# Filler matmuls, a split output projection, and one-hot row picks for the first three experts in a one-core transformer block

## The reference, cut to what matters

```python
mod = silu(c) @ w_ada + b_ada                        # 6 vectors of 1024
h = modulate(rmsnorm(x, norm1_w), shift1, scale1)
proj = h @ w_in                                      # retention q k v g, delta q k v z, a, b
ret = rmsnorm(retention(rotary(q), rotary(k), v)) * silu(g)      # 4 heads of 128
dn  = rmsnorm(gated_delta_rule(conv(q), conv(k), conv(v), g, beta)) * silu(z)   # 4 heads
x = x + gate1 * (concat([ret, dn]) @ w_out)
h2 = modulate(rmsnorm(x, norm2_w), shift2, scale2)
# router: top group of 4, top 2 of its 8 experts (32 experts of 1024 x 512 x 1024)
for each chosen expert e: y = gate * ((silu(h2 @ w1[e]) * (h2 @ w3[e])) @ w2[e])
x = x + gate2 * y;  x = rmsnorm(x)
# second block: pool mixer, then an FFN of 2816 with a causal conv of 3
```

## Time and profile before

| | |
|---|---|
| time, median of 3 runs | 1048.3 us (1047.32 to 1048.72) |
| the profiled execution | 1047.87 us, span 1046.0 us |
| mean granted TensorE clock | 0.948 of full |
| PE busy | 898.8 us (86%) |
| VectorE busy | 365.3 us (35%) |
| ScalarE busy | 199.9 us (19%) |
| moved by DMA | 300.24 MB, mean 287 GB/s |

### The profile page before, as it was taken

The page is one execution under the profiler, slowest core; times in us unless marked ns, Lnnn a source line. Parts: engine busy times, 40 slices in busy tenths (PEclk is TensorE's granted clock), DMA queues, the critical chain, the costliest instruction groups (busy, mean ns, idle before and its releaser), DMA issues.

```text
span 1046.0 us, 11455 instructions
## 1 busy us (share of the span) xinstructions
PE 898.8 (86%) x4665; PEld 545.6 (52%) x4665; DVE 365.3 (35%) x630; ACT 199.9 (19%) x296; POOL 176.1 (17%) x187
## 2 busy tenths in 40 slices
PE   4899999998967979998788887887887279999998
PEld 2687756675433443443233332332332279999987
DVE  1155412232252242221121221211211567888843
ACT  1116212111030000000000000000000335565532
POOL 0001654021020120111101101111001222222300
PEclk9699999997978989999999999999999689999999
DMA  9969227266596999999999999999994884555511
GB/s 344 254 163 262 93 81 238 85 242 258 200 378 227 416 403 401 408 401 401 410 408 409 420 404 401 410 412 414 403 420 192 274 267 151 186 162 187 208 49 41
DMA packets 91348, 300.24 MB, mean 287 GB/s; under 512 B 13451, under 2 KB 37507, under 8 KB 66583
## 3 DMA queue, kind: packets, MB, share of 16 engines
q1 hardware_dynamic: 82295, 286.62, 73.4%
q10 hardware_dynamic: 3872, 8.58, 2.2%
q0 software_dynamic: 5120, 4.22, 1.4%
HBM read 300.43 MB, written 11.53 MB: 298 GB/s over the span
## 4 chain that ended last, share of the span: by engine, by line
PE 60%; DMA 33%; issue 2%; DVE 2%; ACT 2%; POOL 1%; ACTq 0%; POOLq 0%; DVEq 0%
DMA ring<-in_w_dram 19%; DMA arena<-in_w_dram 11%; PE ps L423 9%; PE ps L759 7%; PE ps L843 6%; PE ps L844 6%; PE ps L845 6%; PE ps L412 4%; PE ps L762 4%; PE ps L483 4%; PE ps L782 3%; PE ps L433 2%; PE ps L449 1%; DMA ring<-in_w_ada_dram 1%; PE ps L418 1%
## 5 line engine op out<-in xcount | busy, mean ns | idle before, releaser
L762 PE MATMUL ps<-ring,proj 128*64 128x512 f32 x288 | 129.7, 596 | 25.4 <-DMA ring<-in_w_dram 25.4
L1223 DVE TENSOR_TENSOR proj<-RQ,ps 64x512 f32<-64x512 f32 x32 | 22.1, 690 | 298.2 <-ACT RQ L1562 288.3
L759 PE MATMUL ps<-ring,proj 128*64 128x512 f32 x272 | 124.3, 596 | 0.0
L762 PE MATMUL ps<-arena,proj 128*64 128x512 f32 x224 | 105.4, 619 | 20.3 <-DMA arena<-in_w_dram 20.3
L759 PE MATMUL ps<-arena,proj 128*64 128x512 f32 x240 | 113.9, 617 | 3.6 <-issue 3.6
L1562 ACT ACTIVATE RQ<-ps 64x512 f32<-64x512 f32 x32 | 18.9, 592 | 468.2 <-PE ps L762 468.2
L1792 POOL DMA_INDIRECT pair_scratch<-MX,idx x32 | 32.5, 1014 | 423.7 <-DVE MX L1237 423.7
L843 PE MATMUL ps<-h_h,w_h 128*128 128x256 f32 x352 | 100.4, 285 | 1.6 <-DVE h_l L1319 1.6
L423 PE MATMUL ps<-ring,hT 128*128 128x512 f32 x224 | 100.1, 604 | 0.8 <-ACT hT L1512 0.8
L844 PE MATMUL ps<-h_l,w_h 128*128 128x256 f32 x352 | 100.3, 285 | 0.0
L845 PE MATMUL ps<-h_h,w_l 128*128 128x256 f32 x352 | 100.2, 285 | 0.0
(11 more groups left out here) (286 smaller groups left out, 1374.7 us busy)
## 6 DMA issues: line engine op xcount, KB each, us to landing
ring<-in_w_dram SPq DMA_DIRECT2D x108, 1024.0 KB, 28.2
arena<-in_w_dram SPq DMA_DIRECT2D x84, 1024.0 KB, 27.9
ring<-in_w_ada_dram SPq DMA_DIRECT2D x12, 2048.0 KB, 11.1
ring<-in_ffn_w_in_dram SPq DMA_DIRECT2D x22, 1024.0 KB, 7.8
ring<-in_w_in_dram SPq DMA_DIRECT2D x6, 2048.0 KB, 14.4
ring<-in_ffn_w_out_dram SPq DMA_DIRECT2D x5, 2048.0 KB, 7.6
arena<-in_w_in_dram SPq DMA_DIRECT2D x2, 2048.0 KB, 25.1
ring<-in_w_out_dram SPq DMA_DIRECT2D x2, 2048.0 KB, 7.8
```

What stands on the lines that cost most here:

```text
L759: pe.matmul(ps[0:SLOTS, :], XTe[i % 2][:, k, :], u1[:, k, :], start=(k == 0), stop=(k == 7))
L762: t = pe.matmul(ps[64:64 + SLOTS, :], XTe[i % 2][:, k, :], u3[:, k, :], start=(k == 0), stop=(k == 7))
```

## The change

1. `turn_over(n)` issues n filler matmuls of 128x256 into the next bank. It is put at twelve places: in the first stage, ahead of and between the `ada`, behind the column totals, between the two `logits`, ahead of `rank`, and at two places of `tensor_last`.
2. `column_total` moves 64 columns instead of one.
3. hT is written chunk by chunk, and the first group of `delta_project(0)` waits for each chunk. `ab` is 8 matmuls with AB (padded to 32 columns) stationary and hT moving, four side by side, followed by a copy on VectorE and `ab_sum`. `delta_project(2)` is split: groups 0 and 1 ahead of `ab_sum`, 2 and 3 behind the norms.
4. The retention half of the output projection is done right behind `o1`, into four kept banks; the delta half follows.
5. The router's weights are scaled once (WRS), x1 is copied unscaled, and `logits` are made for each token half, with hT stationary.
6. For experts 0 to 2 nothing is gathered. VectorE makes a one-hot `pick` (token by slot) from ranks, and PE multiplies the h2 rows, from SBUF and at a stride of 8 floats, by it: 16 matmuls of 64 columns. `turn_x(0)` comes ahead of `places(0)` and the gate totals on PE.

```diff
@@ tensor_program @@
+            def turn_over(n):
+                b = banks.next()
+                if banks.count[b]:
+                    pe.wait_ge(bank_free[b], banks.count[b])
+                for _ in range(n):
+                    pe.matmul(PS[b][:, 0:256], ident, C[:, 0:256], start=True, stop=True)
...
                 for c in range(8):
-                    i = pe.matmul(ps[:, c:c + 1], view[:, c, :], sel[:, 0:1], start=True, stop=True)
+                    i = pe.matmul(ps[:, 64 * c:64 * c + 64], view[:, c, :], sel[:, 0:64], start=True, stop=True)
...
+            pe.wait_ge(const_in, 16)
+            turn_over(3)
             ps = take("cols")
...
             pe.wait_ge(crep_ready, 1)
+            turn_over(8)
             ada(0)
+            turn_over(5)
             ada(1)
+            turn_over(2)
             column_total(0)
...
             ada(2)
+            turn_over(5)
             ada(3)
+            turn_over(2)
             column_total(1)
+            turn_over(6)
             banks.kept.clear()
+            def chunk_there(k):
+                c, g = k % 4, k // 4
+                if c < 3:
+                    pe.wait_ge((chunk_ready_a, chunk_ready_v)[g], 2 * c + 2)
+                else:
+                    pe.wait_ge(*drained("x_turned", 0, g))
+                    pe.wait_ge(*drained("x_turned", 1, g))
...
                     for k in range(8):
+                        if seg == 0 and m == 0:
+                            chunk_there(k)
                         i = pe.matmul(ps[:, 0:256], w[:, k, m * 128:(m + 1) * 128], hT[:, k, :],
                                       start=(k == 0), stop=(k == 7))
...
             pe.wait_ge(small_in, SMALL_LOADS)
-            for n in range(2):
-                for k in range(8):
-                    i = pe.matmul(ps[:, 8 * n:8 * n + 8], hT[:, k, tok(n)], AB[:, k, :], start=(k == 0), stop=(k == 7))
+            for r in range(2):
+                for q in range(4):
+                    i = pe.matmul(ps[32 * q:32 * q + 32, 0:256], AB[:, 4 * r + q, :], hT[:, 4 * r + q, :],
+                                  start=(r == 0), stop=(r == 1))
             i.then_inc(*mm.up("ab"))
+            delta_project(2, range(2))
+            ps = take("ab_sum")
+            pe.wait_ge(*drained("ab"))
+            for n in range(2):
+                i = pe.matmul(ps[:, 8 * n:8 * n + 8], ab_turned[:, tok(n)], cst("ab_sum"), start=True, stop=True)
+            i.then_inc(*mm.up("ab_sum"))
             pe.wait_ge(qk_squared, 1)
             for m in (2, 3, 0, 1):
                 ps = take("norm", m)
                 pe.matmul(ps[:, :], ones, SQ[:, 2 * m:2 * m + 2, :], start=True, stop=True).then_inc(*mm.up("norm", m))
-            delta_project(2)
+            delta_project(2, range(2, 4))
...
+            turn_mixed(0, 0)
+            turn_mixed(1, 0)
+            wo = {(n, j): take("wo", n, j, keep=True) for n in range(2) for j in range(2)}
+            for n in range(2):
+                for j in range(2):
+                    w_out(n, j, 0)
+            turn_mixed(0, 1)
             column_total(4)
+            w_out(0, 0, 1)
+            w_out(0, 1, 1)
+            turn_mixed(1, 1)
             ps = take("rb")
...
+                for k in range(8):
+                    i = pe.matmul(ps[:, 0:36], hT[:, k, tok(n)], WRS[:, k, :], start=(k == 0), stop=(k == 7))
+                i.then_inc(*mm.up("logits", n))
+            w_out(1, 0, 1)
+            turn_x1(0)
+            w_out(1, 1, 1)
+            banks.kept.clear()
+            logits(0)
+            turn_over(2)
+            turn_x1(1)
+            turn_over(1)
+            logits(1)
             ada(10)
             ada(11)
+            turn_over(5)
...
+            def routing_rest():
+                places(0)
+                gate_total(10, late_part[0])
+                gate_total(11, late_part[1])
@@ tensor_experts @@
             def turn_x(i):
                 ps = take("turn_x", i)
+                if E is main and i < DIRECT:
+                    if i == 0:
+                        pe.wait_ge(h2_rows, 2)
+                    pe.wait_ge(picked, 2 * i + 2)
+                    for c in range(8):
+                        for n in range(2):
+                            t = pe.matmul(ps[:, c * SLOTS:(c + 1) * SLOTS], MX[:, n, :].rearrange("t (p c) -> t c p", c=8)[:, c, :],
+                                          pick[:, i, n, :], start=(n == 0), stop=(n == 1))
+                    t.then_inc(*E.mm.up("turn_x", i))
+                    return
...
             turn_x(0)
+            if after_first:
+                after_first()
             up(0)
@@ tensor_last @@
+            pe.wait_ge(second_sq, 1)
+            turn_over(6)
             pe.wait_ge(*filled(("late",)))
...
+            turn_over(5)
             for n in range(2):
                 pe.wait_ge(ffn_rows, n + 1)
@@ vector_program @@
-            ve.tensor_copy(ab, full("ab")[:, 0:16].rearrange("p (n h) -> p n h", n=2)).then_inc(*free("ab"))
-            ve.wait_ge(*drained("ab"))
+            ve.tensor_copy(ab_turned, full("ab")[:, 0:256]).then_inc(*free("ab"))
+            ve.tensor_copy(ab, full("ab_sum")[:, 0:16].rearrange("p (n h) -> p n h", n=2)).then_inc(*free("ab_sum"))
+            ve.wait_ge(*drained("ab_sum"))
...
+            ve.tensor_tensor(WRS, WR[:, :, :], modc[:, 3, :].unsqueeze(2).to_broadcast([128, 8, 36]), ALU.mult).then_inc(router_scaled, 1)
...
+            for n in range(2):
+                ve.scalar_tensor_tensor(L[:, n, :], full("logits", n)[:, 0:36], rr[:, n:n + 1], rb, ALU.mult, ALU.add).then_inc(*free("logits", n))
...
             rank = full("rank")[:, 0:64].rearrange("p (n c) -> p n c", n=2)
+            ve.tensor_copy(first_rank, rank[:, :, 0:DIRECT]).then_inc(*vd.up())
+            ve.wait_ge(*vd.now())
+            ve.wait_ge(chosen, 1)
+            for i in range(DIRECT):
+                for n in range(2):
+                    ve.tensor_scalar(pick[:, i, n, :], cst("places")[:, 0:SLOTS], first_rank[:, n, i:i + 1], SM[:, n, i:i + 1],
+                                     ALU.is_equal, ALU.mult).then_inc(picked, 1)
```

More of the change, by code:

```diff
@@ L48, in __init__, with next @@
         self.turn, self.count, self.kept, self.at = 0, [0] * 8, set(), {}
+    def next(self):
+        turn = self.turn
+        while turn % 8 in self.kept:
+            turn += 1
+        return turn % 8
     def take(self, name, keep):
@@ L120, in constants @@
     out["ids"] = np.stack([p, p + 128, p + 256, p + 384], axis=1) - SPARE
+    out["ab_sum"] = (p[:, None] % 32 == np.arange(8)[None, :]) * 1.0
     out["half"] = (p[:, None] >= SLOTS) * 1.0 + 2 * SPARE
@@ L284, in segment @@
             return proj[:, seg, n, :].rearrange(heads4, h=4)
-        fold = cst("masks")[:, 0:64]
-        LE = KT.rearrange("p h d -> p (h d)")[:, 0:256]
+        WRS = S[:, angles_at:angles_at + 288].rearrange("p (c n) -> p c n", c=8)
+        DIRECT = 3
+        pick = hT[:, 4:6, :].rearrange("p a b -> p (a b)")[:, 0:DIRECT * 128].rearrange("p (e n s) -> p e n s", e=DIRECT, n=2)
+        first_rank = small(2 * DIRECT).rearrange("p (n e) -> p n e", n=2)
         v_ffn, v_fin, v_psc, v_pb = gates[:, 1, :], room, gates[:, 0, :], vrow[:, :]
@@ L639, in tensor_program, with turn_mixed, w_out @@
             four(("o1",), lambda h: ATT[:, 1, h, :], lambda h: U1[:, h, :], keep=True)
+            banks.kept.clear()
+            def turn_mixed(n, g):
+                pe.wait_ge((ret_rows, dn_rows)[g], n + 1)
+                four_turned(("m_turned", n, g), lambda c: MX[:, n, (4 * g + c) * 128:(4 * g + c + 1) * 128])
+            def w_out(n, j, g):
+                w = unit(("wo", j), 512)
+                if n == 0 and g == 0:
+                    pe.wait_ge(*filled(("wo", j)))
+                pe.wait_ge(*drained("m_turned", n, g))
+                for k in range(4 * g, 4 * g + 4):
+                    i = pe.matmul(wo[n, j][:, :], hT[:, k, tok(n)], w[:, k, :], start=(k == 0), stop=(k == 7))
+                if g:
+                    i.then_inc(*mm.up("wo", n, j))
+            turn_mixed(0, 0)
[5 more added lines that the diff above has]
+            turn_mixed(0, 1)
             column_total(4)
-            banks.kept.clear()
+            w_out(0, 0, 1)
+            w_out(0, 1, 1)
+            turn_mixed(1, 1)
             ps = take("rb")
@@ L675, in tensor_program, with logits @@
                     four_turned(("x1_turned", n, g), lambda c: eights(X[:, n, :], 4 * g + c))
[L676 to L677 removed]
+            def logits(n):
+                ps = take("logits", n)
+                if n == 0:
+                    pe.wait_ge(router_scaled, 1)
                 pe.wait_ge(*drained("x1_turned", n, 0))
                 pe.wait_ge(*drained("x1_turned", n, 1))
[L680 to L688 removed]
+                for k in range(8):
[4 more added lines that the diff above has]
+            w_out(1, 1, 1)
+            banks.kept.clear()
+            logits(0)
[3 more added lines that the diff above has]
```

(24 more changed lines are left out.)

193 lines of the change are left out of this document (75 added, 118 removed).

## The result

The changed kernel takes 1054.3 us (median of 8 runs, 1051.2 to 1057.3) against 1047.9 (8 runs, 1045.1 to 1049.6) for the kernel before: a ratio of 1.0051, 95% interval 1.0035 to 1.0067. It is slower by 6.4 us; the forecast was 1056.6. So single profiles are read here up to a given mark, and ends are compared by medians.

What follows compares the result with a forecast made beforehand. Bounds: PE to 250 us, a chain with low PE clock to 318, the weight stream from 451 to 797, its queue waiting on PE until 398. Sum at half clock: 1047.9+10.7-2 = 1056.6 us; range 1040 to 1063.

Steps and rivals of the forecast that it cites:

- The front: Start to o1: small loads and a bank wait put project(2,0) 4 us later, column totals return 1; sum +3 us.
- The bank as the stall's cause: In delta_project(2): dn(2,3) takes dn(2,0)'s bank, which VectorE frees late; PE idles about 7 us. No bank wait: 0.12.
- wider column totals: Column totals up to o1: 64 columns may hold the clock, gaining 0 to 1.5 us, 1 taken.
- the fillers are hidden by the waits for data: In the first stage: most fillers run before data is there, so cost nothing; may save 3 us of half clock.
- Output projection and router: From behind o1 to the router's sums: new order ends at 288.5, 7.3 us earlier (bounds 4 and 8.5).
- From router to up(0): Router's sums to expert 0's first matmul: 17.7 us at full clock, 4.7 saved; 20.7 at half clock, 1.7 saved.
- the low clock: PE falls to half clock in the thin picks, slowing up(0), up(1) and down(0) by 2 us each; three to two or better.
- The expert stage: Up(0) to down(0): down(0) late by 1.6 us at full clock, 10.7 at half clock; everything later follows.
- the first two: Cases for the whole: strided picks at half clock, 1056.6 us, chance 0.45; the same at full clock, 1047.5 us, 0.22.
- the first case: Picks at the strided price and half clock: 1056.6 us, own range 1051 to 1062, chance 0.45.
- The sign of the whole: Whole kernel: slower (above 1050.4 us) 0.52, same 0.14, faster 0.34.
- The tail: Fillers before mix and the f_turned groups shorten half-clock stretches: 4.2 us at most, 2 us gain taken.

Runs made afterwards that it cites:

- the packed run: Changed kernel with h2 rows written by ScalarE in chunk order, so the picks' stationary operands are packed: 1040.0 us, 0.9915 of the kernel before.
- the kernel that departs only in the tail: Changed kernel with ScalarE's first cast of FFN weights moved behind the four hT steps in the tail: 1056.5 us, 1.0059 of the kernel before.
- the control: The changed kernel again, unaltered, profiled a second time beside later runs: 1054.5 us, 1.0047 of the kernel before.
- The run with its front 5 us earlier: Changed kernel with ab_sum in ab's bank instead of one of its own: 1053.3 us, 1.0042 of the kernel before.

## Why the prediction was right, point by point

**The front** came out as worked out: ab at 71.39 (71.5 taken), ab_sum done at 81.4 (82), 7.27 us of stall released by the conv read (7.6), the first projection at 103.21 (104.4), o1 3.0 us late (3). The bank as the stall's cause is shown by the run that moves ab_sum. That o1 came out to the tenth is in part luck: the first projection was 1.2 us earlier than worked out, and the 1 us that wider column totals were to give back is not there: from the first projection to the step behind o1 it is 142.95 us after and 142.96 before, and one column or 64 made no difference of more than 0.2 us. One step was wrong: that the fillers are hidden by the waits for data. Those ahead of the first ada pushed it back by 3 us. What they were for they do: without them delta_project(0) ran its first 3.7 us at the lower clock and took 2.1 us more (3 taken). By its end the two cancel.

**Output projection and router.** From the step behind o1 to the sums took 44.8 us, not 52.6: 7.8 won, 7.3 forecast.

**From router to up(0)** took 20.05 us, 2.4 won, against 1.7 for the low clock; the pass of picks took 7.85 us (7.8). That a strided stationary operand and nothing else makes this price is shown by the packed run: 335 against 192 ns a load. The Trainium skill's page SBUF — State Buffer, "Door 1: The DMA port swizzle" (free up to 4 fp32), agrees with both. The rule of the Trainium skill's page TensorE: Matmul & The Clock Gate, "LDWEIGHTS (loading the stationary operand)", a load by its number of columns alone, does not hold here: the same 128 columns took 335 ns at a stride of 8 floats and 192 packed, against 107 by the rule (packed pairs follow each other every 118 ns).

**The expert stage** is the term that was mis-sized: +10.7 us forecast by the low clock, +6.6 measured at the last mark. Up(0) began 1.2 us earlier than taken, and it ran at full clock in 7.0 us, not 8.9. Up(1) (8.9) and down(0) did run as forecast: down(0) took 5.2 us from its first matmul to the next step, against 3.5 before, so 1.8 lost and 2 taken. At its end the lag was 7.3 us, and 0.75 of it was made up in the two later places blocks. That is the 4.1 us. So the case that came true lies between the first two: low clock in two of three places. Why up(0) escaped is not settled. The places matmuls and gate totals stand between it and the thin pass, and the clock was back; but with the same steps there it began at the lower clock (1.12 us) without fillers, with ab_sum in ab's bank, with packed rows, and in the profile of the kernel that departs only in the tail. In that execution all three places were slow, as the first case has it, and its last mark was 8.6 us behind that of the kernel before. The sign of the whole hung on the price of the passes, since two later passes at 6.8 us over the transposes add 13.5 us, more than the 7.2 that up(0) had won.

**The tail** was to give 2 us and gave nothing that can be seen. (Its forecast and the expert stage's were off in opposite directions, by 2 and 4.1 us, so the forecast time is nearer than its terms.) From the first late load to the first FFN matmul it was 33.2 us before (821.33 to 854.57), 32.2 in the control (828.66 to 860.85) and 34.8 in the first profile. The step that failed is that what is won in these stretches of PE is won for the path. Before, the path was PE's there, but ScalarE's cast of FFN weights, for which it waits on a transfer, ended 1 us ahead of mix (ScalarE's and PE's timelines):

```profile
834.72 1.90 ACT L1592 CAST w_h<-ring 128x2048 fp32r<-128x2048 f32 x1 [1.11 <-DMA ring<-in_ffn_w_in_dram]
...
835.92 1.95 PE L818 MATMUL ps<-ring,MX 128*128 128x128 f32 x16
837.71 7.07 PE L830 MATMUL ps<-ring,hT 128*128 128x256 f32 x32
```

After, the fillers did shorten the first part of mix, from 5.2 to 3.65 us, and with that the chain that ended last runs through the transfer and the cast, behind which hT is queued:

```profile
830.76 12.19 DMA ring<-in_ffn_w_in_dram
843.03 1.90 ACT w_h L1662
844.92 0.38 ACT hT L1671
```

In one profile of the same kernel PE then idled 1.31 us and the pooled matmuls took 7.14; in the other it idled 2.20 and they took 8.83. The longer wait goes with the later end of the transfer. Turning ScalarE's order removed this wait but, in the changed kernel, not the time, so what bounds this stage in sum stays open, and with it why a last mark 3 to 4 us earlier (ab_sum's bank, no fillers) did not shorten the end by as much.

**Sum.** 1047.9+6.6+0 = 1054.5, measured 1054.3; with marks that differ by 2 us from one execution to another, so close a fit is luck too.

## What to carry to other kernels

Ask of every stationary operand how it lies in memory: an f32 load at a stride of 8 took 1.7 times a packed one, and writing the rows packed once turned 0.5% slower into 0.85% faster. The writing itself took ScalarE 2.2 us a half instead of 1.15, and since that was over before the picks, the first pass began no later (298.09 against 298.21). A step that is cheap beside its neighbours' waits isn't cheap when it is repeated before the work that frees a full queue's slots: sum all its repeats up to the last point where the queue depends on it. And when a chain is made shorter, look whether the transfer at its end starts earlier into the same backlog: here it then only got longer.

## What the runs showed of the hardware that was not expected

- The last 512 KB of a store of rows took 8.8 us when issued at 297.5, ahead of four weight halves of 1 MB, and 14.2 when issued at 294.5, behind two of them: it ended at 308.7 and, before, at 306.4, so the earlier one even ended later. The DMA share from 280 to 308 was 0.97 and, before, 0.94. That the order of issue makes the difference is not shown apart.
- The clock behind a thin stretch is not the same in every execution of the same instructions. In two profiles of the changed kernel up(0) began with a matmul of 0.64 us and four pairs of up(1) were slow; in the profile of the kernel with the same instructions up to the tail it began with one of 1.12, and six were slow. The run with its front 5 us earlier shows the latter too, so that can't be put down to its edit.
- A pass bound by strided loads doesn't feel the clock, a packed one does. In the changed kernel's first pass PE worked at six matmuls in the us from 299 to 300, at full clock, and at six from 301 to 302, at the lower one; in the packed one at 11 and at seven, and the packed pass took 5.05 us with half of it at the lower clock and 3.79 without.
- A column total, eight matmuls, took 3.9 us with 64 columns moving as with one; its strided loads took 335 ns in both.
- Two profiles of one kernel agree within 0.2 us at every mark to 404 us, and differ by 3.2 at the first FFN matmul; a third execution of the same instructions was 2.1 us later at the last of these marks.
